# A hybrid attention and expert layer on one core: how gate scatters, expert rows and routes are dealt to its stages

## What is computed

```python
def block(xb):                                   # 128 tokens
    q = (xb @ peer_wq).reshape(PEER_BLOCK, PEER_HEADS, 2, PEER_HALF)
    s = jnp.einsum('thcd,hckd->thck', q, peer_sub_keys)
    s1, i1 = lax.top_k(s[:, :, 0], PEER_TOPK)    # 16 of 128
    s2, i2 = lax.top_k(s[:, :, 1], PEER_TOPK)
    ...
    top_s, top_pos = lax.top_k(cand_s, PEER_TOPK)
    experts = jnp.take_along_axis(cand_i, top_pos, axis=-1)
    g = jax.nn.softmax(top_s, axis=-1)
    u = peer_u[experts]
    act = jax.nn.gelu(jnp.einsum('thkd,td->thk', u, xb), approximate=False)
    v = peer_v[experts]
    return jnp.einsum('thk,thkd->td', g * act, v)
h = layer_norm(ALPHA * x + merged @ w_out, ln1_g, ln1_b)
y = layer_norm(ALPHA * h + peer(h), ln2_g, ln2_b)
```

## Time and profile before

| what | value |
|---|---|
| median of 3 runs | 3343.33 us |
| profiled execution, its own time | 3336.23 us |
| span of that execution (first to last instruction) | 3334.5 us |
| mean granted TensorE clock | 0.935 of full |
| TensorE matmul busy | 2952.1 us (89%) |
| VectorE busy | 2391.4 us (72%) |
| ScalarE busy | 1204.9 us (36%) |
| POOL busy | 1502.0 us (45%) |
| moved by DMA | 1096.91 MB, mean 329 GB/s |

### The profile page before, as it was taken

One profiled execution on the slowest core, in us unless ns is written; L12 is line 12 of the kernel. 1 busy time (PEld: TensorE's weight loads), 2 busy tenths in 40 slices (PEclk: granted clock), 3 DMA queues, 4 the chain that ended last, 5 costly groups with the idle time before them and its releaser, 6 DMA issues. The chain is left out here.

```text
span 3334.5 us, 35756 instructions
## 1 busy us (share of the span) xinstructions
PE 2952.1 (89%) x10191; PEld 1638.9 (49%) x10191; DVE 2391.4 (72%) x4846; ACT 1204.9 (36%) x3117; POOL 1502.0 (45%) x1114
## 2 busy tenths in 40 slices
PE   8988989776798898877688899999999999999993
PEld 5755655443445555444445555544444454544441
DVE  0021477797787867888767878778777788787787
ACT  0241233485733334775652422222222222222221
POOL 0000066665673667777888733333323333332330
PEclk9988999887798999888899899999999999999996
DMA  4576689878899999567699999999999999999995
GB/s 142 189 252 220 214 324 351 306 246 277 272 357 387 388 338 332 171 190 217 182 305 315 393 416 415 415 415 415 414 416 415 415 414 414 409 415 409 384 395 211
DMA packets 381189, 1096.91 MB, mean 329 GB/s; under 512 B 91616, under 2 KB 217792, under 8 KB 294848
## 3 DMA queue, kind: packets, MB, share of 16 engines
q0 software_dynamic: 161616, 741.61, 58.7%
q1 hardware_dynamic: 176800, 303.85, 25.6%
q10 hardware_dynamic: 42576, 49.17, 4.3%
HBM read 1031.18 MB, written 62.23 MB: 328 GB/s over the span
## 5 line engine op out<-in xcount | busy, mean ns | idle before, releaser
L467 POOL DMA_INDIRECT expert_rows<-in_experts,picked_index x525 | 613.1, 1168 | 873.0 <-DVE ff_sum L621 749.6
L490 POOL DMA_INDIRECT gates_by_expert<-dense_gate,gate_address x384 | 687.5, 1790 | 213.2 <-issue 114.8
L609 DVE SCALAR_TENSOR_TENSOR expert_rows<-expert_rows,h_tile 128x1024 f32<-128x1024 f32 x557 | 678.3, 1218 | 135.4 <-DMA expert_rows<-in_experts,picked_index 115.8
L621 DVE SCALAR_TENSOR_TENSOR ff_sum<-expert_rows,coefficients,ff_sum 128x1024 f32<-128x1024 f32 x557 | 713.1, 1280 | 31.2 <-ACT coefficients L572 30.4
L1849 PE MATMUL dense_out_ps<-dense_value_rows,dense_weights 128*128 128x512 f32 x1536 | 688.5, 598 | 39.0 <-DVE dense_weights L1927 39.0
L1860 PE MATMUL dense_act_ps<-dense_hT,key_columns 128*128 128x384 f32 x2048 | 691.3, 491 | 19.2 <-DMA key_columns<-in_key_columns 13.2
L1860 PEld LDWEIGHTS dense_act_ps<-dense_hT,key_columns 128*128 128x128 f32 x2048 | 386.5, 191 | 337.4 <-DMA key_columns<-in_key_columns 60.1
L1849 PEld LDWEIGHTS dense_out_ps<-dense_value_rows,dense_weights 128*128 128x128 f32 x1536 | 293.7, 192 | 388.4 <-issue 311.1
L878 PE MATMUL proj_ps<-xT,w_in_block 128*128 128x384 f32 (+1 forms) x1392 | 422.3, 466 | 26.9 <-DMA xT<-in_xT 11.8
L566 ACT ACTIVATE activated<-dots 128x1 f32<-128x1 f32 (+1 forms) x629 | 125.8, 200 | 671.4 <-DVE expert_rows L609 496.5
L878 PEld LDWEIGHTS proj_ps<-xT,w_in_block 128*128 128x128 f32 x1392 | 268.0, 193 | 180.6 <-issue 32.8
(11 more groups left out here) (198 smaller groups left out, 3069.8 us busy)
## 6 DMA issues: line engine op xcount, KB each, us to landing
key_columns<-in_key_columns SPq DMA_DIRECT2D x128, 512.0 KB
dense_value_rows<-in_experts SPq DMA_DIRECT2D x128, 512.0 KB
gates_by_expert<-zeros POOLq DMA_DIRECT2D x12, 2048.0 KB, 21.9
wq_half<-in_peer_wq SPq DMA_DIRECT2D x48, 512.0 KB, 11.4
dense_gates<-gates_by_expert SPq DMA_DIRECT2D x128, 192.0 KB
w_in_block<-in_w_in ACTq DMA_DIRECT2D x18, 1024.0 KB
w_in_block<-in_w_in SPq DMA_DIRECT2D x18, 1024.0 KB
w_out<-in_w_out SPq DMA_DIRECT2D x24, 512.0 KB, 7.4
```

What stands on the lines that cost most here:

```text
L467: pool.indirect_dma_start(to, None, self.a["experts"], bass.IndirectOffsetOnAxis(ap=index[:, k:k + 1], axis=0)).then_inc(got, 16)
L490: pool.indirect_dma_start(self.a["gates_by_expert"], bass.IndirectOffsetOnAxis(ap=self.flat[i][:, k:k + 1], axis=0), self.dgate[i][:, k:k ...
L609: dve.scalar_tensor_tensor(place, place, 1.0, self.h[n % 2][:], ALU.mult, ALU.mult, accum_out=self.dots[:, s % TOPK:s % TOPK + 1]).then_in ...
L621: dve.scalar_tensor_tensor(total, self.slots[self.slot_of[p]][:, D:2 * D], self.coef[:, y % TOPK:y % TOPK + 1], total, ALU.mult, ALU.add). ...
```

## The change

Four things are changed; nothing else in the program.

1. The table `SHARES` has other rows, routes and paces. Made into events, that is (before, then now):

| stage | row steps | route stages | scatters |
|---|---|---|---|
| (0, scores) | 3, 3 | 72, 72 | 5, 5 |
| (1, project) | 44, 44 | 84, 84 | 44, 52 |
| (1, stick) | 24, 26 | 24, 24 | 24, 24 |
| (1, mla_project) | 8, 8 | 12, 12 | 10, 9 |
| (1, mla) | 22, 24 | 24, 24 | 24, 12 |
| (1, merge) | 22, 21 | 0, 0 | 20, 24 |
| (1, scores) | 27, 27 | 36, 48 | 6, 14 |
| (2, project) | 39, 39 | 96, 84 | 55, 61 |
| (2, stick) | 28, 28 | 60, 60 | 60, 60 |
| (2, mla_project) | 7, 7 | 12, 12 | 20, 19 |
| (2, mla) | 25, 28 | 60, 60 | 56, 43 |
| (2, merge) | 16, 16 | 24, 24 | 34, 33 |
| (2, scores) | 28, 28 | 36, 36 | 26, 28 |
| dense | 396, 390 | 252, 252 | 0, 0 |

2. The scatters of a tile's first head (48 of the 384) write instead of add. They are issued in (0, scores) 5, (1, project) 11, (1, scores) 12 and (2, project) 20.
3. At route stage 0 ScalarE now calls `load_scores` with all scores that have been handed to a store so far (`kept`).
4. With the other counts two loads leave the dense stage for (2, scores): one `h_tile` (512 KB) and one pair of `ln2` gains (1 MB). The dense stage fetches 369 expert rows where it fetched 374.

```diff
     SHARES = (
         ((0, "scores"), 3, 1, 6, 8),
-        ((1, "project"), 44, 1, 7, 44), ((1, "stick"), 24, 2, 2, 24), ((1, "mla_project"), 8, 1, 1, 10), ((1, "mla"), 22, 2, 2, 24),
-        ((1, "merge"), 22, 1, 0, 20), ((1, "scores"), 27, 1, 3, 16),
...
+        ((1, "project"), 44, 1, 7, 52), ((1, "stick"), 26, 2, 2, 24), ((1, "mla_project"), 8, 1, 1, 9), ((1, "mla"), 24, 2, 2, 12),
+        ((1, "merge"), 21, 1, 0, 24), ((1, "scores"), 27, 1, 4, 30),
...
             elif e[2] == 0:
+                self.stored |= self.kept
+                self.load_scores(self.nc.scalar)
                 assert self.loaded > e[1], (self.block, e, self.loaded)
...
-        pool.indirect_dma_start(self.a["gates_by_expert"], bass.IndirectOffsetOnAxis(ap=self.flat[i][:, k:k + 1], axis=0),
-                                self.dgate[i][:, k:k + 1], None, compute_op=ALU.add).then_inc(self.added[d], 16)
+        to = bass.IndirectOffsetOnAxis(ap=self.flat[i][:, k:k + 1], axis=0)
+        if h == 0:
+            pool.indirect_dma_start(self.a["gates_by_expert"], to, self.dgate[i][:, k:k + 1], None).then_inc(self.added[d], 16)
+        else:
+            pool.indirect_dma_start(self.a["gates_by_expert"], to, self.dgate[i][:, k:k + 1], None, compute_op=ALU.add).then_inc(self.added[d], 16)
...
                         act.dma_start(kept_at(t, h - 1), stage[n % SB][0:r, :]).then_inc(sc_out[n % SB], 16)
+                        bg.kept.add((t, h - 1))
```

More of the change, by code:

```diff
@@ L183 @@
         ((0, "scores"), 3, 1, 6, 8),
-        ((1, "project"), 44, 1, 7, 44), ((1, "stick"), 24, 2, 2, 24), ((1, "mla_project"), 8, 1, 1, 10), ((1, "mla"), 22, 2, 2, 24),
-        ((1, "merge"), 22, 1, 0, 20), ((1, "scores"), 27, 1, 3, 16),
-        ((2, "project"), 39, 1, 8, 56), ((2, "stick"), 28, 2, 5, 60), ((2, "mla_project"), 7, 1, 1, 20), ((2, "mla"), 25, 2, 5, 56),
-        ((2, "merge"), 16, 1, 2, 34), ((2, "scores"), 28, 1, 3, 30),
+        ((1, "project"), 44, 1, 7, 52), ((1, "stick"), 26, 2, 2, 24), ((1, "mla_project"), 8, 1, 1, 9), ((1, "mla"), 24, 2, 2, 12),
+        ((1, "merge"), 21, 1, 0, 24), ((1, "scores"), 27, 1, 4, 30),
+        ((2, "project"), 39, 1, 7, 61), ((2, "stick"), 28, 2, 5, 60), ((2, "mla_project"), 7, 1, 1, 19), ((2, "mla"), 28, 2, 5, 43),
+        ((2, "merge"), 16, 1, 2, 33), ((2, "scores"), 28, 1, 3, 34),
         ((3, "dense"), 1000, 1, 21, 112),
@@ L239, in __init__ @@
         self.table = None
-        self.stored, self.loaded, self.softmaxed = set(), 0, -1
+        self.kept, self.stored, self.loaded, self.softmaxed = set(), set(), 0, -1
     def lay_out(self):
```

## The result

The changed kernel took 3347.74 us (median of 22 runs), the one before, in runs beside it, 3340.81. The ratio is **1.0029, with a 95% interval of 1.0020 to 1.0037**: 7 to 12 us slower, where I had forecast 11.4 us faster. (The two medians alone give 1.0021; the ratio and its interval are worked out from all the runs.) The profiled execution spans 3346.6 us against 3334.5.

What follows compares the result with a forecast made beforehand. Dense was taken as bound by DMA and PE together, attention by PE, ScalarE and VectorE chains, (2, mla) by POOL. Terms summed to −11.4 us: 3343.3 to 3332 us, range 3312 to 3355.

Steps and rivals of the forecast that it cites:

- scatters' places: Scatter moves: (1, project) +4 us from POOL's pace and a landing wait, (1, mla_project) −4, (2, mla_project) −1, plus (2, mla).
- writes: 48 scatters writing: 0.6 us of POOL saved each, 29 us in all, beside other work except in both `project` stages.
- one route: (1, scores): one route more, 7 us × VectorE's share 0.75, partly in idle time, +4; (2, project): one less, 0.
- −9 for (2, mla): (2, mla): POOL fills the stage; 13 scatters fewer cut VectorE's 20.3 us of row waits, three rows cost 7; −9.
- Dense: Dense stage: 6.82 MB less to load at 415 GB/s, below PE's 54 idle us; −16.4 us (−20 to −8).
- Rival B: (2, mla): PE's 42.0 us wait for `probsT`, not POOL, sets the stage; fewer scatters give nothing; 3345 us, chance 0.25.
- (1, mla_project) −4: (1, mla_project): a 2.95 us landing wait that held the stage's end leaves with one scatter; −4 us (−5 to 0).
- (2, scores), +3: (2, scores): VectorE reaches the first route sooner; a load near 1826 starts it at 1833, stalling 16 us; +3 (0 to +14).
- Rows in the attention stages, +4 and +4: (1, stick) and (1, mla): two rows more in each, 2.34 us of VectorE apiece times its share; +4 us each.
- (1, merge), 0: (1, merge): one row less set against four scatters more; 0 us.
- Rival A: POOL ends the `project` stages: a write costs as much as an add; (1, project) +22, (2, project) +12.5; 3362 us, chance 0.14.
- Rival C: Everything works: (2, mla) −20 for −9, (1, project) −6 for +4; −32 us in all, 3311 us, chance 0.15.

Runs made afterwards that it cites:

- e6: Kernel before with only the changed kernel's scatter paces; all scatters add, rows, routes and load as before: ratio 0.9954 to before.
- e3: Kernel before with the changed kernel's scatter paces and plain writes; rows, routes and load as before: ratio 0.9965 to before.
- e17: Changed kernel with all scatters adding again, all else as in the change: ratio 1.0013 to before.
- e1: Changed kernel with the six rows put back into dense; paces, routes, writes and load kept: ratio 0.9987 to before.
- e2: Kernel before with the six rows moved forward as in the change, and the load; scatters all add, paces and routes as before: ratio 1.0045.
- e13: Changed kernel with the route moved back: 3 routes in (1, scores), 8 in (2, project): ratio 1.0045 to before.
- e8: Kernel before with only the load of scores issued where its route stands on ScalarE: ratio 0.9997 to before.
- e10: e6 with six rows more in (2, scores), 34 for 28, and six fewer in dense: ratio 0.9952 to before.
- e15: Changed kernel with two POOL loads, the gains pair and `h_tile`, moved from the end of (2, scores) into dense: ratio 1.0060 to before.
- e11: e8 with the 12 stages of group 3's first route undivided after 7 rows of (2, scores): ratio 1.0040 to before.
- e12: e6 with (1, merge) back at 20 scatters for 24 and (1, mla) at 16 for 12: 3313.52 us, ratio 0.9934 to before.
- e5: Kernel before with the scatters of each first head as plain writes, nothing else: ratio 1.0025 to before.
- e16: e12 with plain writes for all first heads, as in the change: ratio 0.9965 to before.
- e14: e12 with plain writes for the first heads of tiles 2 and 3 only; tile 1's adds: ratio 0.9934 to before.

## Why the prediction was wrong

The kernel was slower and I said faster. By parts, with the ratios taken times 3340 us (my terms in the middle column):

| part | forecast | measured |
|---|---|---|
| scatters' places | +4 − 4 − 1 − 16 = −17 | −15 (e6) |
| writes | 0 | +4 (e6 to e3), +5 (e17 to changed) |
| six rows | +4 + 4 + 7 + 3 − 16.4 = +2 | +14 (e1 to changed), +15 (e2) |
| one route | +4 | +7 (e3 to e1, with the load); none seen in e13 |
| load | part of the +3 | −1 (e8) |

−15 + 4 + 7 + 14 is the +10 of the result, but that is no check: e6, e3, e1 and the changed kernel follow one another by one part each, so the differences must add up. The +4 of the writes alone is below the 0.0015 that I trust. (The −16 is not a term of my prediction; it is its −9 for (2, mla), with 7 for the rows taken out.) The places' −15 for −17 is partly luck: in e6 (1, project) is 5.6 shorter where I had +4, and (1, merge) 5.7 longer where I had 0.

*What held.* Dense: −16.4 forecast, −14.0 in the change, −15.4 in e10, −16.0 from e8 to e2. That bytes set the length of dense at 415 GB/s fits. Most of these runs also take six rows of VectorE's work out of dense, but e15 moves loads alone: 1.57 MB at 415 GB/s are 3.8 us, and dense grew by 3.9, though that is one profile. Rival B falls: with 13 scatters fewer and the same rows (2, mla) went from 159.1 to 143.4 us (e6), 1.2 us for each; it is 140.9 to 146.3 in the eight profiles with 43 scatters and 25 rows there, and 157.5 to 159.8 in the six with 56 and 25. The rule of the Trainium skill that stood beside it (page "DMA: Bandwidth & Descriptors", section Anatomy of one DMA: many descriptors before their cost shows) does not hold for these scatters of 128 addresses, by the same 1.2 us. (1, mla_project) −4 came as computed; (2, mla) was −9 in this profile and −3 to −5 in those of e13, e15 and e17, whose counts there are the same.

*The step that failed most: (2, scores), +3.* I had the mechanism, and its bound of +14, but took the low end because "the load may now go ahead of the store that stood before it", near 1826 in the old time line. It did not: it waits for the landing of its own store, 5.9 us after it, and the route starts 37.5 to 40.0 us into the stage in every profile. The right sum was to keep 38.6 fixed: my +3 was three rows' 7.0 left for later less the 4.4 by which I let the route start earlier, and without the 4.4 it is +7; e11 gives +6.2 for that alone. (My "near 1817" for VectorE's arrival doesn't fit its own terms: 1837.42 − 5.08 − 7.0 is 1825.3. VectorE came 21.2 us into the stage, 1820 in the old time line, and idled 17.15 us, near the 16 I had. From e8 to e11 that idle time rose by 11.3 and the stage by 6.2, so the idle time is not the price either.) A second part is at the stage's end, where the gains pair and `h_tile`, which I had counted only as 1.57 MB leaving dense, stand in POOL's queue ahead of the last rows. I booked their gain and not their cost; e15 shows the two cancel, 4.0 against 3.9. Together that is 10.2 of the +11.6; but e1, with all but the rows as in the change, has the stage at 111.1, and of the 14.6 from there some 4 stay open.

*Rows in the attention stages, +4 and +4.* They cost 5.4 and 6.8, and from e1 to the changed kernel 2.4 us a row in (1, stick) and 3.6 in (1, mla), where I took 2.34 × 0.87. In a chained stage I should have taken the full price and the gap behind it. In (2, mla) a row cost 1.4 between these two profiles, and 3.6 from e8 to e2. Six rows at 2.4 to 3.6 us are 14 to 22 us against 16.4: this move had little or nothing to win, before the stall. e10 shows no more than that at another place.

*(1, merge), 0.* It is 4.7 longer with one row less (and not longer in e17). I did not read POOL there; from e6 to e12 the stage follows POOL's queue. It was the cheapest gain that was left out: e12.

*The writes, 0.* That a write "lies beside other work", or helps inside the terms of the two `project` stages, was argued from POOL's time alone. The price was right (0.99 us) and the resource wrong: nothing in my text asked what the transfer does to the engines that `w_in` shares. The writes cost 8 us in e5, and PE's wait for `w_in` went from 1.5 to 4.3 us there. That is a missing step, not a mis-sized one.

*Rival A* forecast slower, with the wrong place. More scatters do not lengthen (1, project); e6 shortens it by 5.6 with eight more. Its point of decision, a write that costs POOL as much as an add, never came. *Rival C*'s two gains are there when only the paces change: −5.6 in (1, project) for its −6, and −15.7 in (2, mla) for its −20 (e6). The writes took the first back and the rows some of the second.

## What to carry to other kernels

A unit of background work moved between two stages has a price at both ends; if the receiving stage is a chain and the giving one is bound by bytes, compare the two prices (here 2.4 to 3.6 us a row against 2.6) before counting the gain. When work ahead of an item is moved earlier, ask first what time the item's own input is ready: here it was fixed, so the work moved turned into a wait. A cheaper transfer on one queue can starve a more urgent one on another where the engines are full.

## What the runs showed of the hardware

An indirect scatter of 128 addresses of 4 bytes costs POOL 0.99 us as a write and 1.60 as an add. The adding one has 112 more packets below 512 B, and still in the 5 us window above it left the weights' queue 60.3% of the engines' time and the writing one 32.0%. I had expected the lighter instruction to be the lighter transfer for everyone.

A stop that I can't explain stands in three profiles, e13, e15 and e16: in (0, scores), whose program is the same as in the changed kernel or e3, ScalarE waits 8.38 us (in e16) before a copy for which it waits 3.48 in the changed kernel, and 5.19 before the next copy of scores. e16, then the changed kernel:

```profile
439.79 0.40 ACT L1743 COPY peer_qT<-peer_q_ps 128x288 f32<-128x288 f32 x1 [8.38 <-remote]
...
446.81 0.37 ACT L1756 COPY score_stage<-peer_score_ps 128x256 f32<-128x256 f32 x1 [5.19 <-remote]
```

```profile
434.94 0.40 ACT L1745 COPY peer_qT<-peer_q_ps 128x288 f32<-128x288 f32 x1 [3.48 <-PE peer_q_ps L1719]
```

The profile names no engine for it. It makes (0, scores) 97 us for 87. If the other executions of those three kernels have it too, their ratios are up to 0.003 too high to be read as the cost of their edits; no row tells. All three write tile 1's first head, as do seven profiles without it. All three also ran on one chip, where e14, in which tile 1's first head adds, does not have it, and no other kernel that writes there is on record for that chip. Whether the stop belongs to the writes, to the chip or to both stays open.
